# The last residual of a four-part decoder step: x stored ahead, and the scaled tiles added to it in memory by GpSimd's transfers

## What is computed

```
def rmsnorm(x, g):
    xf = x.astype(jnp.float32)
    y = xf * lax.rsqrt(jnp.mean(xf * xf, axis=-1, keepdims=True) + EPS)
    return (y * g.astype(jnp.float32)).astype(x.dtype)
...
        x = x + rmsnorm(y, norm_post[layer, 1])
        x = x + 0.5 * rmsnorm(swiglu(rmsnorm(x, norm_pre[layer, 2]), ffn_in[layer, 1], ffn_out[layer, 1]), norm_post[layer, 2])
    return x, jnp.stack(states), jnp.stack(convs), c_new, pe_new
```

## Time and profile before

| | |
|---|---|
| time, median of 3 runs (lowest to highest) | 1454.01 us (1452.28 to 1454.56) |
| the profiled execution: its own time | 1454.49 us |
| the profiled execution: span from first to last instruction | 1452.8 us |
| TensorE busy | 1426.9 us, 98% of the span |
| VectorE busy | 899.9 us, 62% |
| ScalarE busy | 748.4 us, 52% |
| GpSimd busy | 159.7 us, 11% |
| moved by the DMA engines | 221.90 MB, mean 153 GB/s |

### The profile page before, as it was taken

One profiled execution on the slowest core, in us unless ns is written; L12 is line 12 of the kernel. 1 busy time (PEld: TensorE's weight loads), 2 busy tenths in 40 slices (PEclk: granted clock), 3 DMA queues, 4 the chain that ended last, 5 costly groups with the idle time before them and its releaser, 6 DMA issues.

```text
span 1452.8 us, 29593 instructions
## 1 busy us (share of the span) xinstructions
PE 1426.9 (98%) x11036; PEld 1359.5 (94%) x11036; DVE 899.9 (62%) x1494; ACT 748.4 (52%) x1227; POOL 159.7 (11%) x226
## 2 busy tenths in 40 slices
PE   9999999999999999999999999999999999999997
PEld 9999998999977999999999999999877699999997
DVE  6655535988977686554367555449755548655434
ACT  6555425678654465554256555336533336555423
POOL 0111000000210011110001111001144301111000
PEclk9999999999999999999999999999999999999999
DMA  6444433443421334444424444443599653444441
GB/s 241 160 156 152 145 144 125 145 145 122 149 95 63 127 118 168 144 146 152 156 97 174 147 155 156 156 145 137 181 297 286 217 174 102 162 153 159 148 145 65
DMA packets 50632, 221.90 MB, mean 153 GB/s; under 512 B 6689, under 2 KB 23074, under 8 KB 28530
## 3 DMA queue, kind: packets, MB, share of 16 engines
q1 hardware_dynamic: 39026, 190.61, 37.4%
q0 software_dynamic: 6192, 24.64, 5.0%
q10 hardware_dynamic: 5328, 5.51, 1.2%
HBM read 213.96 MB, written 6.77 MB: 152 GB/s over the span
## 4 chain that ended last, share of the span: by engine, by line
PE 92%; DVE 5%; ACT 1%; issue 1%; DMA 0%; DVEq 0%; ACTq 0%
PE psum L276 15%; PE psum L271 15%; PE psum L272 15%; PE psum L369 8%; PE psum L370 8%; PE psum L371 8%; PE psum L2560 2%; PE psum L2518 2%; DVE w_lo L259 1%; PE psum L1434 1%; PE psum L2389 1%; PE psum L298 1%; PE psum L2522 1%; PE psum L2534 1%; PE psum L293 1%
## 5 line engine op out<-in xcount | busy, mean ns | idle before, releaser
L259 DVE TENSOR_TENSOR w_lo<-raw,w_hi 128x2048 fp32r<-128x2048 f32 x161 | 373.3, 2319 | 293.9 <-ACT w_hi L252 293.7
L252 ACT ACTIVATE w_hi<-raw 128x2048 fp32r<-128x2048 f32 x156 | 299.0, 1917 | 352.3 <-PE psum L371 207.7
L271 PE MATMUL psum<-h_hi,w_hi 128*128 128x320 f32 x1520 | 452.3, 311 | 0.6 <-DVE arena L1189 0.6
L272 PE MATMUL psum<-h_lo,w_hi 128*128 128x320 f32 x1520 | 449.4, 309 | 0.0
L271 PEld LDWEIGHTS psum<-h_hi,w_hi 128*128 128x128 f32 x1520 | 285.7, 188 | 2.2 <-DVE arena L1189 0.9
L272 PEld LDWEIGHTS psum<-h_lo,w_hi 128*128 128x128 f32 x1520 | 285.9, 188 | 0.8
L276 PE MATMUL psum<-h_hi,w_lo 128*128 128x320 f32 x1520 | 254.7, 310 | 0.0
L276 PEld LDWEIGHTS psum<-h_hi,w_lo 128*128 128x128 f32 x1520 | 231.4, 188 | 0.3 <-DVE w_lo L259 0.3
L370 PE MATMUL psum<-hid_lo,w_hi 128*128 (+1 forms) x704 | 217.6, 309 | 0.0
L369 PE MATMUL psum<-hid_hi,w_hi 128*128 (+1 forms) x704 | 217.6, 309 | 0.0
L371 PE MATMUL psum<-hid_hi,w_lo 128*128 (+1 forms) x704 | 217.6, 309 | 0.0
(11 more groups left out here) (436 smaller groups left out, 1944.5 us busy)
## 6 DMA issues: line engine op xcount, KB each, us to landing
raw<-wts SPq DMA_DIRECT2D x162, 1024.0 KB, 4.8
h_plain<-cache_t POOLq DMA_DIRECT2D x44, 160.0 KB, 3.7
h_plain<-cache_t SPq DMA_DIRECT2D x44, 160.0 KB, 3.6
arena<-s POOLq DMA_DIRECT2D x4, 1024.0 KB, 7.3
sgs<-arena POOLq DMA_DIRECT2D x4, 1024.0 KB, 4.2
marena<-cache_t POOLq DMA_DIRECT2D x20, 160.0 KB, 3.9
marena<-cache_t SPq DMA_DIRECT2D x20, 160.0 KB, 3.5
raw<-cache_c SPq DMA_DIRECT2D x16, 128.0 KB, 3.9
```

What stands on the lines that cost most here:

```text
L252: act.activation(w_hi[c0 % 2][:, :], raw_of(c0, pair)[:, :], ACT.Copy).then_inc(hi_ready, 1)
L259: eng.tensor_tensor(w_lo[c0 % 2][:, :], raw_of(c0, pair)[:, :], w_hi[c0 % 2][:, :].bitcast(F32), ALU.subtract).then_inc(lo_ready, 1)
L271: pe.matmul(outs[n], wtile(w_hi, c0, n * K + k), src_hi(k), start=(k == 0), stop=False)
L272: pe.matmul(outs[n], wtile(w_hi, c0, n * K + k), src_lo(k), start=False, stop=False)
```

## The change

The output buffer is filled with x before the last FFN's result is known: once x of the sub-layer before is complete, GpSimd issues one store of all of x to y_t. In the last `residual_dve` the eight additions are gone, and only the scaling is left. GpSimd waits until a pair of tiles of y is scaled and issues a transfer with `accum_op=ALU.add`, which adds the pair to what stands in y_t. Before the first of the four it waits until the fill has landed, and at the end until all four have. SyncE's four stores are gone. Two semaphores are renamed and shared otherwise, with no change for their other users.

```diff
             if pre is None:
-                add(0)
-                scale(1)
                 for m in range(1, KT):
-                    if m + 1 < KT:
-                        scale(m + 1)
-                    add(m)
+                    scale(m)
                 return
...
-            for m in range(0, KT, 2):
-                sp.wait_ge(x_ready, 5 * KT + m + 2)
-                sp.dma_start(io["y_t"][:, m:m + 2, :], x[:, m:m + 2, :]).then_inc(third_then_out, 16)
-            sp.wait_ge(third_then_out, 16 + 16 * (KT // 2))
...
             second_high_pool(pool, BASE["ffn3"] + 1)
+            pool.wait_ge(x_ready, 5 * KT)
+            pool.dma_start(io["y_t"], x).then_inc(kv_then_out, 16)
             ffn_pool(pool, 3)
+            pool.wait_ge(kv_then_out, 48)
+            for m in range(0, KT, 2):
+                pool.wait_ge(y_scaled, 5 * (KT + 1) + m + 3)
+                pool.dma_start(io["y_t"][:, m:m + 2, :], y[:, m:m + 2, :], accum_op=ALU.add).then_inc(kv_then_out, 16)
+            pool.wait_ge(kv_then_out, 48 + 16 * (KT // 2))
```

More of the change, by code:

```diff
@@ L223, in build @@
         hid_hi_ready, hid_lo_ready = sem("hid_hi_ready"), sem("hid_lo_ready")
-        third_then_out = sem("third_then_out")
+        third_landed = sem("third_landed")
         def landed(c):
@@ L246, in split_hi @@
             if isinstance(pair, int) and c0 + 2 * pair == 2:
-                act.wait_ge(third_then_out, 16)
+                act.wait_ge(third_landed, 16)
             else:
@@ L2000, in build @@
             "kv_taken", "kv_sq", "latent_summed", "latent_r", "kv_step", "kv_pe", "kv_ready"))
-        kv_out = sem("kv_out")
+        kv_then_out = sem("kv_then_out")
         kp_raw, kp_c, kp_s, kp_b = (y[0:ROPE, n, :] for n in range(4))
@@ L2090, in kv_pool @@
             pool.wait_ge(kv_ready, 4)
-            pool.dma_start(io["ckv_t"], ckvT[:, :, :]).then_inc(kv_out, 16)
-            pool.dma_start(io["kpe_t"], kpeT[0:ROPE, :]).then_inc(kv_out, 16)
+            pool.dma_start(io["ckv_t"], ckvT[:, :, :]).then_inc(kv_then_out, 16)
+            pool.dma_start(io["kpe_t"], kpeT[0:ROPE, :]).then_inc(kv_then_out, 16)
         NP = DEC_B // 2
@@ L2876, in _ @@
                     load_quarter(sp, c, q)
-            sp.dma_start(raw_third[:, :], io["wts"][2, :, :]).then_inc(third_then_out, 16)
+            sp.dma_start(raw_third[:, :], io["wts"][2, :, :]).then_inc(third_landed, 16)
             sp.dma_start(con[:, :], io["consts"]).then_inc(con_landed, 16)
@@ L2957, in _ @@
             pool.wait_ge(pack_out, 16)
-            pool.wait_ge(kv_out, 32)
+            pool.wait_ge(kv_then_out, 32)
         @block.scalar
```

## The result

The changed kernel takes 1467.17 us (median of 4 runs, 1466.19 to 1468.88) against 1454.18 us before (4 runs): 13.0 us more, a ratio of 1.0095 with a 95% interval of 1.0079 to 1.0111. It is slower, by far more than the forecast 1.4 us, and outside the range of 1451.5 to 1461.5.

The account below looks back on a forecast made before the run. VectorE's scalings and additions, then the last store, bound the tail. Removing 3.2 us of additions, then four adding transfers of 1.8 us from 1445.97 plus 0.45, with a slower start, made 1.4 us later: 1455.4 us, range 1451.5 to 1461.5.

Parts of the forecast that it names:

- What bounds the kernel now: Tail: VectorE alone scales and adds from 1443.73 to 1450.21, then the last store lands at 1452.4; span ends 0.4 us later.
- The sum: End of kernel: 1445.97 + 4 x 1.8 + 0.45 = 1453.6, 1.2 us later than 1452.4; with a slower start, 1.4 us.
- What is removed: Last residual on VectorE: eight additions of 0.40 us, 3.2 us, all on the path.
- GpSimd's start and issue: Tail: first adding transfer starts at 1444.87, data from 1445.97; issue 0.54 us if about as long as a plain one's.
- How long one adding transfer moves: Output transfers at the end: bounded between 0.90 and 2.6 us each, far end 6 us; middle of 1.8 us taken.
- the likeliest case: Last four transfers: 1.8 us each, giving a median of 1455.4, own range 1454.5 to 1456.9; chance 0.45.
- The fill: Before the last FFN: 1280 KB move for 3.3 us, overlapping the next weight load by 0.3 us with 3.0 us room; free.
- the first: Rival, at the tail: adding transfers are slow, mostly 3 to 8 us lost; 2.2 us each decides it; chance 0.30.
- The second: Rival, at the tail: transfers add at a store's pace, gaining 2.7 us at most; median 1451.3 to 1452.5; chance 0.20.
- The third: Rival, at the tail: VectorE keeps GpSimd from issuing until the last scaling ends; median 1457.8; chance 0.05.
- What would show it: Profile after: scalings end near 1447.0, 1.8 us per transfer, last landing near 1453.8, last wait GpSimd's, no longer ScalarE wait.

Follow-up runs that it names:

- experiment 4: Kernel before without the eight last additions and without the fill, SyncE storing scaled y plainly (output lacks x): 1450.38 us, ratio 0.9972.
- experiment 3: Changed kernel with accum_op left out, so GpSimd's four last transfers store plainly (output lacks x): 1461.56 us, ratio 1.0043.
- experiment 8: Changed kernel with two adding transfers of 640 KB instead of four of 320 KB: 1465.75 us, ratio 1.0082.
- experiment 2: Kernel before with a wait at the end of GpSimd's program until ScalarE has squared the last tile: 1454.43 us, ratio 1.0004.
- experiment 5: Changed kernel with SyncE instead of GpSimd waiting for the landing of the four adding transfers: 1461.69 us, ratio 1.0044.
- experiment 7: Kernel before with GpSimd issuing two plain 1 MB loads after the last addition, SyncE waiting for them: 1465.98 us, one run.

## Why the prediction was wrong

By the tail, from the first multiplication with r_post to the end of the span, the 12.1 us divide as follows. Additions gone: 3.4 us less (experiment 4). GpSimd in place of SyncE: the last plain landing comes 1.3 us later than there (7.3 against 6.0, experiments 3 and 4). Adding: 5.1 us (12.4 against 7.3). Drain: 9.5 us from the last landing to the end in place of 0.4, 9.1 us. The sum is 12.1.

- *What bounds the kernel now*: right up to its last step, which failed. "The span ends 0.4 us later" was true of the kernel before, whose last wait is SyncE's. The sum carried it over to a kernel whose last wait is GpSimd's. The drain of 9505 ns stood in the trace of before at 1365.2, without a cost there, because it began over 87 us ahead of the end. No rival had it. That is 9.1 of the 11.6 us by which the forecast (1.4) missed the measured loss (13.0). Had I read what GpSimd still does at the end of its program, the sum would have been some 10.5 us.
- *What is removed*: right. VectorE was done 3.3 us sooner, where I had 3.2.
- *GpSimd's start and issue*: the start near 1.9 us into the tail came at 2.1; the issue "in about the time of a plain one" was wrong, 0.92 to 1.45 us against 0.54. This did not set the time: the issues overlap and start within 2.2 us, and with half as many (experiment 8) the data moved for 8.1 us instead of 8.7.
- *How long one adding transfer moves*: the likeliest case took 1.8 us each, 182 GB/s, from two reads on one side of a DMA engine. In the steady part it was 183 GB/s on average, so this size was right. But the last landing came 12.4 us into the tail instead of 10.8 (the forecast's 1453.8, with the tail's start at 1442.98), 1.6 us of the miss. The sum lacked the slow start and a slow end. By the slices, the first 1.8 us moved 164 KB, which takes 0.9 us less at 183 GB/s, and the last 0.9 us moved 49 KB, 0.6 us less at that rate; the data also began 0.15 us late (3.34 us into the tail instead of 3.19). The Trainium skill (Collectives: The Full Stack, section on the bandwidth ceiling) has half the rate of a copy. The trace agrees if the copy is a plain store of 320 KB over its 0.90 us, 364 GB/s; against the 430 to 450 of experiment 3's slices, 183 is less than half.
- *The fill*: right, nothing.
- *The rivals*: the first (slow adding, 2.2 us a transfer as its border) named the outcome, slower, but not the cause of most of it; the data's 8.7 us are 2.2 us a transfer, just at its border, and the last landing came 3.0 us later than before (12.4 against 9.4). The second never came. The third did not show either: data began to move at 1447.5, while VectorE was scaling until 1448.05. By the Trainium skill (SBUF — State Buffer, section "Who interferes with whom") tensor_tensor locks only what GpSimd reads and does not hold up its DMAs, which the page gives as in part inferred; the trace agrees, since experiment 3's issues took 0.54 to 0.60 us beside the same scalings.
- *What would show it*: the list told me to look for the last wait on GpSimd, and it was there; what follows that wait was not on the list.

What remains of the miss, 0.9 us (11.6 less 9.1 and 1.6), is the difference between the medians' 13.0 us and the tails' 12.1; the granted clock ahead of the tail moves single executions by more than that.

## What to carry to other kernels

Read the rows at the very end of every engine's program, those that cost nothing too: work that is moved to an engine at the end brings that engine's drain with it. GpSimd should be done with its program some 10 us before the last landing; in experiment 2 its drain then cost nothing. Its own transfers should have landed some 5 us before the end, as inferred from experiments 5 and 7; no run tests that distance by itself. An addition made by a DMA queue moved its bytes at less than half the rate and started slowly, so it pays only where there is time behind it; an idle TensorE can add a tile in PSUM with one fp32 matmul for x and one for y, 0.54 us from one to the next, and took 1.2 us off this tail.

## What the runs showed of the hardware

- GpSimd's drain at the end of a program took 9.05 to 9.6 us in every kernel where none of its transfers was long under way, whether the last had landed 150 to 290 us before or just then; SyncE's took 7 ns, TensorE's and ScalarE's 0.5 to 2.3 us, VectorE's 0.8 to 2.3 us.
- With transfers of GpSimd's under way it took 12.8 us (plain, one run) and 14.2 us (adding), and ended 4.5 to 4.6 us after the last landing.
- An adding transfer to memory from GpSimd ran at 183 GB/s on average (320 KB each) and about 200 (640 KB each) after a start of some 2 us mostly below 130 and with a last 0.7 to 0.9 us below 90, plain ones of the same data at 430 to 450 GB/s; its issue took 0.92 to 1.45 us against 0.54.
- TensorE's granted clock was 1.00 of 2.4 GHz in one profile from 300 to 400 us, and fell to 0.50 for 5 us of it in another, over the same instructions; by this and a like dip near 385 us the tail starts 3.7 us later (1440.46 against 1444.16).
